# Low parts of the projection weights formed on VectorE instead of GpSimd, and one memset that waits longer, in a two-layer hybrid decoder kernel

## The chip, the cores and the metric

The kernel runs on one core of a Trainium2 chip. The metric is the device time of one execution in microseconds (us), lower is better. The kernel before takes 945.29 us, the median of 3 runs (944.92 to 946.22).

The engines are named as the profile names them: PE (TensorE, its weight loads are PEld), DVE (VectorE), ACT (ScalarE), POOL (GpSimd) and SP (SyncE, which here only issues transfers).

## What is computed

Two layers on 256 tokens of width 1024. Each layer projects a modulated, normalised input with one matrix, runs four kinds of mixer on slices of the result, projects back, and then runs a grouped mixture of experts:

```python
c_act = jax.nn.silu(c)
for l in range(DEPTH):
    mod = (c_act @ w_ada[l] + b_ada[l])[:, None, :]
    sh1, sc1, g1, sh2, sc2, g2 = jnp.split(mod, 6, axis=-1)
    u = layer_norm(x) * (1.0 + sc1) + sh1
    (a_q, a_kv, a_kr, m_q, m_k, m_v, m_i, m_f, m_o,
     c_b, c_c, c_h, d_q, d_k, d_v) = split_cols(u @ w_in[l])
    ...
    mix = jnp.concatenate([y_a, y_b, y_c, y_d], axis=-1) @ w_out[l]
    x = layer_norm(DN_ALPHA * x + g1 * mix) * ln1_g[l] + ln1_b[l]
    u2 = layer_norm(x) * (1.0 + sc2) + sh2
    ffn = grouped_moe(u2, w_router, b_router, w1[l], w3[l], w2[l])
    x = layer_norm(DN_ALPHA * x + g2 * ffn) * ln2_g[l] + ln2_b[l]
```

## The kernel before

Every engine has its own list of instructions, written out by hand in the order in which it runs them; semaphores tie the lists together. In the text a semaphore name such as `hi_ready` stands for a count that one engine raises and another waits for.

**The projection `u @ w_in`.** The 2912 columns of `w_in` are cut into 12 tiles (`W_IN_TILES`, line 61), numbered 0 to 11: tile 1 has 96 columns, tile 5 has 264, the others 256. A tile is 128 partitions x 8 blocks (k) x its columns, some 1 MB, and lands in one of 4 slots of `w_ring`. The product is made in split precision: each tile is split in a high part `w_hi` (the f32 value rounded to the type fp32r, a copy on ACT, `high_part`, line 534) and a low part `w_lo` = tile - `w_hi`, which is written over the tile itself. PE then makes, for each half of a tile (a step) and each k, three matmuls: hi x hi, hi x lo, lo x hi (`w_step`, line 1321), 24 per step and 48 per tile. Before the first step of tile n it waits for `hi_ready` and `lo_ready` of that tile. The input is split likewise: `low_part(t)` on DVE (line 868) makes `u_lo` for each of the two blocks of 128 tokens, and the first two steps wait for it.

**Where the low parts are made.** In the kernel before POOL makes them, tile after tile:

```python
for n in range(NW_IN):                                   # line 504
    pool.wait_ge(*Y(hi_ready, n + 1))
    cols = (slice(None), slice(None), slice(0, W_IN_TILES[n][1]))
    nc.gpsimd.tensor_tensor(w_lo[n % W_SLOTS][cols], w_ring[n % W_SLOTS][cols],
                            w_hi[n % W_HI][:].bitcast(F32)[cols], ALU.subtract).then_inc(lo_ready, 1)
    if n == 5:
        root(1, slice(0, 4))
```

POOL also forms inverse square roots for every normalisation (`root`, line 489, `entry_root`, line 494).

**The modulation.** `c_act @ w_ada[l]` is not done on PE. `w_ada[l]` comes in 48 tiles of 128 x 1024, and for each DVE does one `scalar_tensor_tensor` that multiplies the tile by a column of c and adds it into the sums `mod_acc` (128 x 6144) (`ada_step`, line 763; the profile's line L767). I call one such instruction a modulation step. In layer 0 the first 16 steps (shift1 and scale1) come ahead of everything; a `drain` then releases PE (`acc_first`), which sums over the partitions with 32 small matmuls (`first_columns`, line 1308), and only then can the input be modulated and split and the projection start. The other 32 steps, numbered q = 0 to 31, stand in `ada_rest(lo, hi)` (line 879) between DVE's own work for the mixers: 6, then 8, 6, 3, 3 and 6. After the last, `acc_rest` releases the `gate_rows` matmuls on PE, early in the attention. The sums of layer 1 are made during layer 0's expert stage (`next_ada`, line 1087): POOL clears `mod_acc` (line 518) once PE has read layer 0's columns (`cols2`), ACT loads the bias into it (line 704), and DVE waits for that bias before the first step (line 1171).

**The transfers.** SP issues all weight loads in one fixed order (lines 419 to 475). In the projection of layer 0 the order is: load of tile n of `w_in`, then the two tiles of `w_ada` for steps q = 2(n-1) and 2(n-1)+1; behind tile 11 follow q = 20 to 31 and then `w_out` (`ADA_BETWEEN`, line 80). The load of tile n waits until PE has begun tile n-3, because only then is its slot free (`w_free`); a tile of `w_ada` waits until the step 9 places earlier is done (`ada_free`). In the expert stage the loads of the next layer's `w_ada` (3 slots there) stand ahead of and between the expert weights, on the same queue.

**DVE's order in the projection.** Mixer A's latents: squares summed (line 900), rotation of the shared key (814 to 820), steps, product with the inverse root (line 914, raises `lat_ready`, for which PE waits behind tile 7 in `turn_latents`, line 1350), rotation of mixer D's q and k, steps, a copy (line 930), the gate rows of mixer B (lines 934 to 945, with ACT's Exp and Ln in between; the last raises `rows_ready`, for which `project_latents`, line 1367, waits behind tile 9), steps, copies and a rotation, steps, convolution.

**Ahead of the router.** In `post_norm` and `normalise` (lines 822 and 785) DVE ends the first half of a layer: `normalise(t)` writes `xn` and raises `xn_ready`; PE turns it (`turn_x`) and multiplies by the router's weights.

**Between the layers.** For each block of tokens DVE does `post_norm`, `entry_variance` (line 839), waits for POOL's `entry_root`, and does `normalise` (lines 1273 to 1280), after which PE can start layer 1.

## Time and profile before

| | us |
|---|---|
| median of 3 runs | 945.29 |
| the profiled execution | 947.67 |
| span of its instructions | 945.5 |
| PE busy | 805.6 (85%) |
| DVE busy | 453.1 (48%) |
| ACT busy | 173.5 (18%) |
| POOL busy | 147.5 (16%) |
| POOL busy with the low parts (L508, 24 instructions) | 113.4 |

The page of the profile gives the busy time of each engine, a strip of 40 slices of the span, the chain of work that ended last, and the costliest groups of instructions. Behind it stand views that can be asked for a stretch of time. A row of the timeline reads: start us, duration us, engine, line, operation, out<-in, shape, xcount, and in brackets the idle time of the engine before it and what ended that. The duration of a row with xcount over 1 is that of the whole group, idle time inside it included. A row of the table of windows reads: stretch, its length, then the busy time of PE, PEld, DVE, ACT and POOL with their counts, the mean granted clock of PE (1.00 is full speed), the busy share of the DMA engines, and GB/s. A row of the view of one source line gives the least, median and greatest duration of one instruction in ns, and the first and last start. A row of the view of DMA issues ends in the median us from issue to landing.

### The profile page before, as it was taken

To read this page: it belongs to the slowest core of one execution; us is meant where nothing else is said; L and a number is where in the kernel's file an instruction comes from. 1 tells how busy PE (TensorE), PEld (TensorE's weight loads), DVE (VectorE), ACT (ScalarE), POOL (GpSimd) and SP (SyncE) were. 2 spreads that over 40 slices of the span, in tenths; PEclk is the share of its full clock that TensorE was granted. 3 is DMA by queue.
4 is the path that set the end of the run, shared out by engine and by line. 5 is a ranking of instruction groups with operands and counts; after the bars stand their busy time and mean duration, and the time that the engine had idled before them with its cause. 6 is when DMAs were issued, how large, how long until landed. Compare 5 with 4: busy or idle time off the path is not lost.

```text
span 945.5 us, 12491 instructions
## 1 busy us (share of the span) xinstructions
PE 805.6 (85%) x4922; PEld 670.3 (71%) x4922; DVE 453.1 (48%) x768; ACT 173.5 (18%) x357; POOL 147.5 (16%) x56
## 2 busy tenths in 40 slices
PE   1389387979779888898999699899796999999996
PEld 1389375658758767777866599767695888878872
DVE  6699987453757234433217668445365011111106
ACT  0155132410122000000001445333002300000000
POOL 3278510000300000000001678100010000000001
PEclk8589799999769899999998799999895999999998
DMA  9969477700028789988770255460001167767731
GB/s 355 343 215 337 151 266 242 317 1 1 1 80 282 296 344 397 379 348 352 315 268 3 80 179 180 163 282 2 0 1 45 42 265 294 289 266 268 287 156 46
DMA packets 71902, 192.34 MB, mean 203 GB/s; under 512 B 9383, under 2 KB 41383, under 8 KB 63659
## 3 DMA queue, kind: packets, MB, share of 16 engines
q1 hardware_dynamic: 66024, 184.73, 52.3%
q10 hardware_dynamic: 5830, 6.94, 2.2%
q8 instruction: 34, 0.56, 0.2%
q14 instruction: 14, 0.11, 0.0%
HBM read 190.60 MB, written 1.05 MB: 203 GB/s over the span
## 4 chain that ended last, share of the span: by engine, by line
PE 65%; DVE 14%; issue 8%; DMA 7%; ACT 1%; DVEq 1%; POOL 1%; SPq 1%; POOLq 0%; ACTq 0%
PE bank L1625 21%; PE bank L1658 10%; PE bank L1526 6%; DVE mod_acc L767 4%; DMA e_ring<-in_w 4%; PE bank L1340 4%; PE bank L1342 4%; PE bank L1305 2%; PE bank L1609 2%; DMA ada_ring<-in_w_ada 2%; PE bank L1673 1%; PE bank L1541 1%; DVE tmp L786 1%; PE bank L1461 1%; PE bank L1471 1%
## 5 line engine op out<-in xcount | busy, mean ns | idle before, releaser
L1625 PE MATMUL bank<-arena,e_ring 128*128 (+1 forms) x2048 | 242.4, 281 | 17.4 <-DMA e_ring<-in_w 9.4
L1625 PEld LDWEIGHTS bank<-arena,e_ring 128*128 128x128 f32 x2048 | 239.0, 197 | 19.3 <-issue 19.1
L492 POOL TENSOR_TENSOR rstd<-var,neg_half 128x1 f32<-128x1 f32 (+2 forms) x16 | 19.7, 1234 | 710.9 <-DVE var L783 562.6
L508 POOL TENSOR_TENSOR w_lo<-w_ring,w_hi 128x2048 fp32r<-128x2048 f32 (+2 forms) x24 | 113.4, 4737 | 72.2 <-ACT w_hi L540 72.2
L767 DVE SCALAR_TENSOR_TENSOR mod_acc<-ada_ring,c_col,mod_acc 128x1024 f32<-128x1024 f32 x66 | 91.7, 1412 | 64.0 <-DMA ada_ring<-in_w_ada 63.7
L1658 PE MATMUL bank<-e_ring,arena 128*128 128x512 f32 x256 | 115.3, 593 | 2.3 <-DVE arena L1208 2.3
L1203 DVE TENSOR_TENSOR arena<-arena,bank 128x256 f32<-128x256 f32 x32 | 13.4, 420 | 167.5 <-PE bank L1642 167.3
L1658 PEld LDWEIGHTS bank<-e_ring,arena 128*128 128x128 f32 x256 | 46.2, 191 | 48.5 <-issue 48.5
L1342 PE MATMUL bank<-w_hi,u_hi 128*128 128x256 f32 (+2 forms) x224 | 66.3, 296 | 8.7 <-DVE u_lo L871 8.7
L718 ACT ACTIVATE arena<-bank 128x256 f32<-128x256 f32 x32 | 12.3, 383 | 326.3 <-PE bank L1625 326.3
L767 DVE SCALAR_TENSOR_TENSOR mod_acc<-ada_open,c_col,mod_acc 128x1024 f32<-128x1024 f32 x30 | 71.4, 2434 | 0.4 <-DMA ada_open<-in_w_ada 0.4
L1342 PE MATMUL bank<-w_lo,u_hi 128*128 128x256 f32 (+2 forms) x224 | 65.4, 292 | 0.0
L1342 PE MATMUL bank<-w_hi,u_lo 128*128 128x256 f32 (+2 forms) x224 | 65.2, 291 | 0.0
L1526 PE MATMUL bank<-w_ring,uT 128*128 128x256 f32 x256 | 55.7, 380 | 1.7 <-issue 1.7
L1526 PEld LDWEIGHTS bank<-w_ring,uT 128*128 128x128 f32 x256 | 48.5, 190 | 8.6 <-issue 2.1
L1342 PEld LDWEIGHTS bank<-w_hi,u_hi 128*128 128x128 f32 x224 | 45.1, 201 | 9.6 <-issue 7.7
L540 ACT ACTIVATE w_hi<-w_ring 128x2048 fp32r<-128x2048 f32 (+2 forms) x24 | 43.8, 1841 | 36.5 <-DMA w_ring<-in_w_in 24.7
L1305 PE MATMUL bank<-ones,mod_acc 128*128 128x32 f32 x128 | 30.8, 412 | 21.6 <-DVEq L865 21.6
L1340 PE MATMUL bank<-u_hi,w_hi 128*128 128x256 f32 x160 | 47.1, 294 | 0.0
L1305 PEld LDWEIGHTS bank<-ones,mod_acc 128*128 128x128 f32 x128 | 30.8, 334 | 22.2 <-DVEq L865 21.8
L1340 PE MATMUL bank<-u_hi,w_lo 128*128 128x256 f32 x160 | 45.4, 284 | 0.0
L1340 PE MATMUL bank<-u_lo,w_hi 128*128 128x256 f32 x160 | 45.4, 283 | 0.0
(240 smaller groups left out, 1078.4 us busy)
## 6 DMA issues: line engine op xcount, KB each, us to landing
e_ring<-in_w SPq DMA_DIRECT2D x96, 1024.0 KB, 7.9
ada_ring<-in_w_ada SPq DMA_DIRECT2D x66, 512.0 KB, 6.5
w_ring<-in_w_in SPq DMA_DIRECT2D x20, 1024.0 KB, 5.7
ada_open<-in_w_ada SPq DMA_DIRECT2D x30, 512.0 KB, 7.6
w_ring<-in_w_out SPq DMA_DIRECT2D x8, 1024.0 KB, 6.9
w_ring<-in_w_in SPq DMA_DIRECT2D x2, 1056.0 KB, 5.9
ln_gb<-in_ln_g ACTq DMA_DIRECT2D x4, 512.0 KB, 5.0
ln_gb<-in_ln_b ACTq DMA_DIRECT2D x4, 512.0 KB, 6.2
```

Of the source, the lines that this page charges most:

```text
L492: nc.gpsimd.tensor_tensor(rstd[:, cols], var[:, cols], neg_half[:, cols], ALU.pow).then_inc(rstd_ready, 1)
L508: nc.gpsimd.tensor_tensor(w_lo[n % W_SLOTS][cols], w_ring[n % W_SLOTS][cols], w_hi[n % W_HI][:].bitcast(F32)[cols], ALU.subtract).then_inc ...
L540: nc.scalar.activation(w_hi[n % W_HI][:, :, 0:width], w_ring[n % W_SLOTS][:, :, 0:width], ACT.Copy).then_inc(hi_ready, 1)
L767: V.scalar_tensor_tensor(out=part, in0=ada_open[slot][:], scalar=k_col, in1=part, op0=ALU.mult, op1=ALU.add).then_inc(ada_free, 1)
L1203: V.tensor_tensor(sgate[:, j % 2, :].rearrange("p (c n) -> p c n", c=2), silu[:, j % 2, :].rearrange("p (c n) -> p c n", c=2), gate, ALU.m ...
L1305: mm = pe.matmul(bank[b][:, c0:c0 + MOD_W], cols, ones[:, 0:MOD_W], start=True, stop=True)
L1340: mm = pe.matmul(dst[:, 0:S], wt[:, k, half * P:(half + 1) * P], u[:, k, :], start=first, stop=final)
L1342: mm = pe.matmul(dst[:, 0:width], u[:, k, half * P:(half + 1) * P], wt[:, k, 0:width], start=first, stop=final)
L1526: mm = pe.matmul(bank[2 * t + s // 2][:, (s % 2) * 256:(s % 2 + 1) * 256], uT[:, k, t * P:(t + 1) * P], w[:, k, 0:256], start=(k == 0), st ...
L1609: mm = pe.matmul(bank[k][:, :], xn[:, t, k:k + KC * (P - 1) + 1:KC], to_slot[:, t, :], start=(t == 0), stop=(t == NT - 1))
L1625: mm = pe.matmul(bank[j % 2][:, (2 * q + c) * CAP:(2 * q + c + 1) * CAP], w[:, k, c * P:(c + 1) * P], moving, start=(k == 0), stop=(k == K ...
L1658: mm = pe.matmul(bank[4 + half][:, :], hT[:, j % 2, c * CAP:(c + 1) * CAP], w[:, c, half * 512:(half + 1) * 512], start=(j == 0 and c == 0 ...
```

## The change

The loop on POOL is gone. DVE gets a function `w_low(of, n)` that does the same subtraction for tile n, with the same waits and semaphore, and calls it 12 times per layer at fixed places between its other work; the low part of tile 0 of layer 1 is made ahead of the last `normalise` of layer 0. `ada_rest` is cut into smaller pieces, with a `w_low` between them. On ACT the high part of tile 1 moves ahead of `evict_x`. On POOL the first `root` of a layer no longer stands behind tile 5's low part, and the memset of `mod_acc` also waits for `xn_ready` of both blocks of tokens.

```diff
--- before.py
+++ after.py
@@ -501,20 +501,14 @@
                 entry_root(t + 1, t)
             for l in range(DEPTH):
                 Y, M = layer_view(l), moe_sems[l]
-                for n in range(NW_IN):
-
-                    pool.wait_ge(*Y(hi_ready, n + 1))
-                    cols = (slice(None), slice(None), slice(0, W_IN_TILES[n][1]))
-                    nc.gpsimd.tensor_tensor(w_lo[n % W_SLOTS][cols], w_ring[n % W_SLOTS][cols],
-                                            w_hi[n % W_HI][:].bitcast(F32)[cols], ALU.subtract).then_inc(lo_ready, 1)
-                    if n == 5:
-                        root(1, slice(0, 4))
+                root(1, slice(0, 4))
                 root(2, slice(0, 8))
                 for t in range(NT):
                     root(3 + 2 * t, slice(t, t + 1))
                     root(4 + 2 * t, slice(t, t + 1))
                 if l < DEPTH - 1:
                     pool.wait_ge(*Y(cols2, 1))
+                    pool.wait_ge(*Y(xn_ready, NT))
                     nc.gpsimd.memset(mod_acc[:], 0.0).then_inc(acc_zero, 1)
                 for t in range(NT):
                     root(7 + t, slice(t, t + 1))
@@ -559,9 +553,9 @@
                 if l > 0:
                     act.wait_ge(*layer_view(l - 1)(moe_done, 2 * NT))
                 high_part(l, 0)
+                high_part(l, 1)
                 evict_x(0, 0)
-                for n in range(1, W_HI):
-                    high_part(l, n)
+                high_part(l, 2)
 
 
                 def param(dst, src):
@@ -852,6 +846,13 @@
                 dve.wait_ge(entry_rstd, t + 1)
                 normalise(t).then_inc(entry_ready, 1)
 
+            def w_low(of, n):
+
+                dve.wait_ge(*of(hi_ready, n + 1))
+                cols = (slice(None), slice(None), slice(0, W_IN_TILES[n][1]))
+                V.tensor_tensor(w_lo[n % W_SLOTS][cols], w_ring[n % W_SLOTS][cols],
+                                w_hi[n % W_HI][:].bitcast(F32)[cols], ALU.subtract).then_inc(lo_ready, 1)
+
             for l in range(DEPTH):
                 Y, M = layer_view(l), moe_sems[l]
                 if l < 1:
@@ -863,6 +864,8 @@
                         ada_step(n % ADA_OPEN, n // ADA_OPEN + 1, c_col[:, n // 2:n // 2 + 1], n % 2)
                 if l == 0:
                     dve.drain().then_inc(acc_first, 1)
+                    w_low(Y, 0)
+                    w_low(Y, 1)
                 dve.wait_ge(*Y(mod_cols, 1))
                 mod_columns(0, 7)
                 def low_part(t):
@@ -887,7 +890,12 @@
                                 dve.wait_ge(ada_free, ADA_OPEN + n - 3)
                             ada_step(n % ADA_OPEN, n // ADA_OPEN + 1, c_col[:, q // 4:q // 4 + 1], 2 + q % 4)
 
-                ada_rest(0, 6)
+                if l > 0:
+                    w_low(Y, 1)
+                w_low(Y, 2)
+                ada_rest(0, 4)
+                w_low(Y, 3)
+                ada_rest(4, 6)
                 if l > 0:
                     dve.drain().then_inc(acc_rest, 1)
 
@@ -906,7 +914,11 @@
                 rotate(zA[:, :, 320:352].unsqueeze(2), kf[:, :, :].rearrange("p t (h c) -> p t h c", h=NH)[:, :, :, NOPE:QK],
                        1, NH).then_inc(v, 1)
                 chain[0] += 1
-                ada_rest(6, 14)
+                w_low(Y, 4)
+                ada_rest(6, 10)
+                w_low(Y, 5)
+                ada_rest(10, 14)
+                w_low(Y, 6)
                 dve.wait_ge(*Y(rstd_ready, 1))
                 for t in range(NT):
                     for q, (c0, n, g) in enumerate(((0, Q_LORA, C_GQ), (Q_LORA, KV_LORA, C_GKV))):
@@ -925,7 +937,11 @@
                 dve.wait_ge(v, chain[0])
                 qk = zD[:, :, 0:512].rearrange("p t (h r) -> p t h r", h=16)
                 rotate(qk, qk, 16).then_inc(d_roped, 1)
-                ada_rest(14, 20)
+                w_low(Y, 7)
+                ada_rest(14, 17)
+                w_low(Y, 8)
+                ada_rest(17, 20)
+                w_low(Y, 9)
                 dve.wait_ge(*Y(lat_t, 2))
                 V.tensor_copy(pT1, bank[1][0:Q_LORA - P, 0:S]).then_inc(lat_dve, 1)
 
@@ -934,6 +950,7 @@
                 link(V.tensor_scalar(rows[:, 0, :], bank[2][0:NH, S:2 * S], cur[0:NH, C_BF:C_BF + 1], None, ALU.add))
                 link(V.tensor_scalar(rows[:, 1, :], rows[:, 0, :], -1.0, None, ALU.mult))
                 V.tensor_tensor(rows[:, 1, :], rows[:, 0, :], rows[:, 1, :], ALU.min).then_inc(f_ready, 1)
+                w_low(Y, 10)
                 dve.wait_ge(*Y(lf_ready, 1))
                 link(V.scalar_tensor_tensor(out=rows[:, 0, :], in0=rows[:, 0, :], scalar=0.0, in1=rows[:, 1, :],
                                             op0=ALU.min, op1=ALU.subtract))
@@ -944,6 +961,7 @@
                 link(V.tensor_tensor_scan(rows[:, 3, :], ones_row, rows[:, 1, :], 0.0, ALU.mult, ALU.max))
                 V.tensor_tensor(rows[:, 2, :], rows[:, 2, :], rows[:, 3, :], ALU.add).then_inc(rows_ready, 1)
 
+                w_low(Y, 11)
                 ada_rest(20, 23)
 
                 for t in range(NT):
@@ -1276,6 +1294,8 @@
                     if l < DEPTH - 1:
                         dve.wait_ge(*Y(x_done, t + 1))
                         entry_variance(t, 3 * NT * (l + 1) + 3 * t)
+                        if t == NT - 1:
+                            w_low(layer_view(l + 1), 0)
                         dve.wait_ge(entry_rstd, NT * (l + 1) + (t + 1))
                         normalise(t).then_inc(entry_ready, 1)
 
```

**The order on DVE, layer 0, between the rotation of the shared key and the product with the inverse root.** The names: `mod_acc` rows are modulation steps, the others write mixer data; `w_lo_53` and so on are slots of the ring (53 is that of tiles 0, 4, 8; 54 of 1, 5, 9; 55 of 2, 6, 10; 56 of 3, 7, 11). Before:

```order
L820 TENSOR_TENSOR arena<-tmp 128x8x32
L767 SCALAR_TENSOR_TENSOR mod_acc<-ada_open_71,c_col,mod_acc 128x1024
L767 SCALAR_TENSOR_TENSOR mod_acc<-ada_open_72,c_col,mod_acc 128x1024
L767 SCALAR_TENSOR_TENSOR mod_acc<-ada_open_73,c_col,mod_acc 128x1024
L767 SCALAR_TENSOR_TENSOR mod_acc<-ada_open_74,c_col,mod_acc 128x1024
L767 SCALAR_TENSOR_TENSOR mod_acc<-ada_open_75,c_col,mod_acc 128x1024
L767 SCALAR_TENSOR_TENSOR mod_acc<-ada_ring,c_col,mod_acc 128x1024 x3
L914 SCALAR_TENSOR_TENSOR arena<-arena,rstd,cur 128x192
```

and now:

```order
L814 TENSOR_TENSOR arena<-tmp 128x8x32
L853 TENSOR_TENSOR w_lo_53<-w_ring_49,w_hi_64 128x8x256
L761 SCALAR_TENSOR_TENSOR mod_acc<-ada_open_71,c_col,mod_acc 128x1024
L761 SCALAR_TENSOR_TENSOR mod_acc<-ada_open_72,c_col,mod_acc 128x1024
L761 SCALAR_TENSOR_TENSOR mod_acc<-ada_open_73,c_col,mod_acc 128x1024
L761 SCALAR_TENSOR_TENSOR mod_acc<-ada_open_74,c_col,mod_acc 128x1024
L853 TENSOR_TENSOR w_lo_54<-w_ring_50,w_hi_65 128x2112
L761 SCALAR_TENSOR_TENSOR mod_acc<-ada_open_75,c_col,mod_acc 128x1024
L761 SCALAR_TENSOR_TENSOR mod_acc<-ada_ring,c_col,mod_acc 128x1024 x3
L853 TENSOR_TENSOR w_lo_55<-w_ring_51,w_hi_63 128x8x256
L926 SCALAR_TENSOR_TENSOR arena<-arena,rstd,cur 128x192
```

The low parts of tiles 4, 5 and 6 now stand among the eight steps q = 6 to 13, on the same engine; a step that waits for its data holds up the low part behind it.

**The order on DVE where layer 0 ends.** Before:

```order
L842 BN_STATS st<-x_sb 128x6 x2
L844 BN_AGGR mv<-st 128x2
L846 TENSOR_SCALAR var<-mv 128x1
L786 TENSOR_SCALAR tmp<-x_sb,mv,rstd 128x1024
L800 COPY mcol<-bank 128x8
```

and now:

```order
L836 BN_STATS st<-x_sb 128x6 x2
L838 BN_AGGR mv<-st 128x2
L840 TENSOR_SCALAR var<-mv 128x1
L853 TENSOR_TENSOR w_lo_53<-w_ring_49,w_hi_63 128x8x256
L780 TENSOR_SCALAR tmp<-x_sb,mv,rstd 128x1024
L794 COPY mcol<-bank 128x8
```

The low part of layer 1's first tile came in between the variance, which POOL's `entry_root` waits for, and the normalisation, which waits for that root.

## Rows read from the trace of the kernel before

**Rows 1.** Table of windows: the projection of layer 0 in two pieces, its expert stage.

```profile
54.00:100.00 46.00, 44.16 (x360) 43.96 (x360) 45.93 (x24) 20.24 (x26) 39.59 (x9) 0.96 0.93 312
100.00:117.00 17.00, 3.92 (x19) 3.51 (x20) 16.96 (x17) 2.10 (x2) 8.36 (x2) 0.60 0.29 89
278.40:495.00 216.60, 198.09 (x1252) 163.02 (x1251) 82.33 (x113) 15.24 (x28) 0.00 (x0) 0.96 0.86 329
```

**Rows 2.** Waits of the first 170 us: who waited for whom, total, times, longest.

```profile
PE bank L1353 <- DVE arena L914: 14.8, 1, 14.8
```

**Rows 3.** Timeline of layer 0's projection: a step, and DVE beside a low part.

```profile
81.80 5.64 DVE L767 SCALAR_TENSOR_TENSOR mod_acc<-ada_open,c_col,mod_acc 128x1024 f32<-128x1024 f32 x1
...
124.13 4.56 POOL L508 TENSOR_TENSOR w_lo<-w_ring,w_hi 128x2048 fp32r<-128x2048 f32 x1 [15.77 <-ACT w_hi L540]
...
124.28 0.46 DVE L934 TENSOR_SCALAR rows<-bank,cur 4x256 f32<-4x256 f32 x1
124.78 4.06 DVE L935 TENSOR_SCALAR rows<-rows 4x256 f32<-4x256 f32 x1
```

**Rows 4.** Groups by shape, 54 to 163 us: busy, mean ns, idle before.

```profile
L767 DVE SCALAR_TENSOR_TENSOR mod_acc<-ada_open,c_col,mod_acc 128x1024 f32<-128x1024 f32 x20 | 55.0, 2804 | 0.0
L767 DVE SCALAR_TENSOR_TENSOR mod_acc<-ada_ring,c_col,mod_acc 128x1024 f32<-128x1024 f32 x12 | 23.2, 1988 | 0.0
```

**Rows 5.** One source line, 278 to 495 us: steps while POOL is idle.

```profile
L767 DVE SCALAR_TENSOR_TENSOR mod_acc<-ada_ring,c_col,mod_acc x48: 1280/1284/1287, 278.4 to 452.0; 128x1024 f32<-128x1024 f32 x48
```

**Rows 6.** Timeline of DVE, layer 0: two-input instructions and steps with POOL idle.

```profile
47.55 1.23 DVE L871 TENSOR_TENSOR u_lo<-arena,u_hi 128x1024 fp32r<-128x1024 f32 x1 [0.36 <-ACT u_hi L552]
...
114.30 0.68 DVE L815 TENSOR_TENSOR tmp<-arena,const 128x512 f32<-128x512 f32 x1
...
116.77 7.26 DVE L767 SCALAR_TENSOR_TENSOR mod_acc<-ada_open,c_col,mod_acc 128x1024 f32<-128x1024 f32 x6
```

**Rows 7.** Timeline of the opening: step 15 of the first 16, and PE's column sums.

```profile
29.04 5.01 POOL L508 TENSOR_TENSOR w_lo<-w_ring,w_hi 128x2048 fp32r<-128x2048 f32 x1 [17.39 <-ACT w_hi L540]
...
29.69 5.44 DVE L767 SCALAR_TENSOR_TENSOR mod_acc<-ada_open,c_col,mod_acc 128x1024 f32<-128x1024 f32 x1
...
36.43 7.82 PE L1305 MATMUL bank<-ones,mod_acc 128*128 128x32 f32 x32 [21.63 <-DVEq L865]
```

**Rows 8.** Timeline of ACT: evictions of projection steps, the last in layer 0.

```profile
75.47 0.39 ACT L631 ACTIVATE arena<-bank 128x256 f32<-128x256 f32 x1 [2.45 <-PE bank L1342]
...
81.15 0.39 ACT L631 ACTIVATE arena<-bank 128x256 f32<-128x256 f32 x1 [2.46 <-PE bank L1342]
...
148.27 0.38 ACT L631 ACTIVATE arena<-bank 128x256 f32<-128x256 f32 x1 [2.45 <-PE bank L1340]
```

**Rows 9.** DMA issues, 54 to 100 us, and below it 15 to 44 us.

```profile
ada_open<-in_w_ada SPq DMA_DIRECT2D x10, 512.0 KB, 6.4
...
ada_open<-in_w_ada SPq DMA_DIRECT2D x7, 512.0 KB, 9.8
```

**Rows 10.** Timeline ahead of layer 0's router, and layer 1's quiet normalisation.

```profile
252.82 5.22 POOL L518 MEMSET mod_acc<- 128x6144 f32 x1 [0.50 <-PE bank L1305]
...
253.07 5.51 DVE L786 TENSOR_SCALAR tmp<-x_sb,mv,rstd 128x1024 f32<-128x1024 f32 x1
...
267.29 0.25 ACTq L704 DMA_DIRECT2D mod_acc<-in_b_ada  x1
...
711.99 0.81 DVE L786 TENSOR_SCALAR tmp<-x_sb,mv,rstd 128x1024 f32<-128x1024 f32 x1
```

**Rows 11.** Timeline between the layers.

```profile
504.69 1.52 POOL L492 TENSOR_TENSOR rstd<-var,neg_half 128x1 f32<-128x1 f32 x1 [246.66 <-DVE var L783]
509.44 0.55 POOL L497 TENSOR_TENSOR rstd<-var,neg_half 128x1 f32<-128x1 f32 x1 [3.23 <-DVE var L846]
...
520.79 4.97 DVE L786 TENSOR_SCALAR tmp<-x_sb,mv,rstd 128x1024 f32<-128x1024 f32 x1 [0.66 <-POOL rstd L497]
...
535.49 0.39 PE L1342 MATMUL bank<-w_hi,u_hi 128*128 128x256 f32 x1 [0.79 <-DVE u_lo L871]
```

## Prediction

> **What bounds the kernel now.** I first read the page's chain of work that ended last, then the table of windows for the stretches where that chain changes engine, then the waits, then single rows of the timeline. Three stretches matter.
>
> The first is the projection of layer 0. Between 54 and 100 us PE and DVE are both busy nearly all the time [rows 1], so the shares don't say who leads. From 100 to 117 us they do: PE worked 3.9 us of 17, DVE all 17 [rows 1], and the longest single wait of PE is 14.8 us for DVE's product L914 [rows 2]. DVE leads. But DVE's busy time is mostly a stall in disguise. A modulation step there shows 5.64 us [rows 3]; with POOL idle the same instruction takes 1.28, 48 times over [rows 5]. In the opening POOL's low part runs from 29.04 to 34.05, and the step that starts at 29.69 ends at 35.13, 1.1 us after it [rows 7]: they don't share, they take turns, one whole instruction each. Even an instruction on 4 partitions, started 0.65 us after a low part of 4.56 us, took 4.06 us, to that one's end, while its neighbour that reads PSUM took 0.46 beside it [rows 3]. So it is a lock on something that an instruction with its inputs in SBUF needs and one with its large input in PSUM doesn't.
>
> The Trainium skill ("SBUF — State Buffer", Who interferes with whom) says so: VectorE and GpSimd share one pair of ports, a DVE instruction with two SBUF inputs contends with a GpSimd instruction that reads SBUF, and the later one blocks fully. The trace agrees with it.
>
> The second stretch is the normalisation ahead of layer 0's router (5.51 us beside the memset, 0.81 in layer 1 where there is no memset [rows 10]), the third the one between the layers (4.97 us [rows 11]). PE waits for both.
>
> **Prices.** A step costs DVE 7.26 / 6 = 1.2 us when POOL is quiet [rows 6]. The subtraction of 128x2048 is not in DVE's trace. The same operation on 1024 columns takes 1.23 us, a two-input one on 512 takes 0.68 [rows 6], which is 0.55 per 512: 0.68 + 3 x 0.55 = 2.3 us, my estimate (2.4 for tile 5, 0.9 for tile 1). Bounds: 2.2 below (four times the 0.55), 5.0 above, what it costs POOL in the opening [rows 7]; I take 2.3, since it lies on DVE's own rows.
>
> In DVE's queue from 54 to 163 us the 32 steps take 55.0 + 23.2 = 78.2 us [rows 4]; they will take 32 x 1.2 = 38.4. Added are the low parts of tiles 2 to 11, 9 x 2.3 + 2.4 = 23.1. L935 loses 3.6 of its 4.06. Net 20 us less work on DVE. What of it PE gets has to be walked through, since DVE will now be waiting for tiles and PE for low parts.
>
> **Part 1, the opening.** The last step but one takes 5.44 us, beside POOL's 5.01 [rows 7]. Alone it is over after 1.3. The last step's tile must have landed too; it was issued a good microsecond after the one before, so I take 3.9 of the 4.2 us. The low parts of tiles 0 and 1 (3.2 us on DVE) hide under PE's 7.8 us of column sums [rows 7], and ACT's high part of tile 1, now ahead of its evictions, needs 0.9 there; if the cover went, each would cost its length once. Then `low_part` of the second block loses its own wait: 0.7 more for the second step. PE is 4.6 us ahead: it begins tile 1 at 52.4, tile 2 at 57.8, tile 3 at 65.1 (the slow piece in tile 2 I leave as it is).
>
> **Part 2, the loop in the projection.** A tile takes PE 81.15 - 75.47 = 5.68 us [rows 8]. Tiles of w_ada land 6.4 us after issue [rows 9], those of w_in, issued just ahead, no later; the group behind tile n is issued when PE begins tile n-3, the w_ada tiles about 1.3 us later. DVE from 48.8: low part 2, four steps, low part 3 (58.2), two steps, squares and rotation, low part 4 (64.8), steps 6 to 9 (69.6), low part 5 (72.0), then step 10, which waits for its tile (72.3), and step 12 and 13, which land at 77.9 and 78.5 and end at 80.3; low part 6 at 82.6. PE wanted tile 6 at 82.2. Product, rotation (5.1) and low part 7: 90.0, where PE wanted 88.3. Low part 8 at 95.9, PE arrives with its transposes at 97.0; steps 17 to 19 and low part 9 at 101.8, PE arrives at 102.7. Tile 9 ends at 108.4; the gate rows are ready at 111.2 (ACT's Exp and Ln behind the high part of tile 11), inside the 5.1 us of latent projections. Low parts 10 and 11 are done at 105.7 and 113.5. Tiles 10 and 11 end at 124.9. Before, the last eviction starts at 148.27 [rows 8]. **Gain 23.3 us**, of which 4.6 is part 1: the 14.8 us wait is gone and 2.1 us of small waits for low parts 6 and 7 stay. The steps 20 to 31 stand behind that with 1.2 us each, as before by the last six; gate_rows comes 23.3 earlier too.
>
> **Part 3, the memset.** The normalisation falls from 5.51 to 0.81 us [rows 10]: **4.7 us**, PE waits for it alone. The memset then runs 5.2 us from 0.8 us later in the chain. Behind it are POOL's later roots (20 us and more away) and ACT's bias load, which is issued at 267.29, 9 us after the memset's end [rows 10]; it will be issued 4.7 earlier with the router, so 3.6 us of cover are left. DVE's evictions meanwhile read PSUM; the row with 0.46 us says they aren't held. If they were, up to 3 us come back.
>
> **Part 4, between the layers.** The low part of tile 0 is issued on DVE right behind the variance, just before POOL's root can start. A root behind which DVE has a long two-input product takes 1.52 us, one behind which DVE has nothing 0.55 [rows 11]: I read it as the lock seen from POOL. So low part 2.3, root 0.55, normalisation 0.8: with 0.1 us of signals it ends 3.8 us after the variance, against 5.7 now (the normalisation ends at 525.76, the root before it starts 0.6 us ahead of it): **1.9 us** gained, not the 4.2 that the lock costs. Then the second `low_part` is quick and the 0.79 us wait [rows 11] goes: **0.8**. In layer 1 a low part of 2.3 us per 5.7 us tile beside DVE's other work never reaches PE; its projection is PE's own already.
>
> **The rest** moves along. The expert stage of layer 0 is fed by a queue of loads whose first wait is for the first modulation step of layer 1, so it starts as much earlier as that step; steps there run with POOL idle and stay 1.28 [rows 5].
>
> **Sum:** 23.3 + 4.7 + 1.9 + 0.8 = 30.7 us. The profiled execution, 947.67, becomes 917.0; it lies 2.4 above the median of the runs, so the median 945.29 becomes **914.6 us**.
>
> **Rivals.**
>
> A. The loop is slower than I walk it (chance 0.14). Low parts now stand behind steps that wait for transfers, and those are issued by PE's progress. If w_ada tiles land after 9.8 us, the median of the crowded opening [rows 9], step 13 ends at 83.0, low part 6 at 85.3 (3.1 us late), and low part 9 comes 2 us late again: 5 us back, 919.5. With 13 us it is 926. For it: DMA is 0.93 busy there [rows 1]. Against: 6.4 is the median of just that stretch [rows 9].
>
> B. The steps are long of themselves, and POOL only keeps time with them (0.03). Then DVE, busy 45.93 of 46 us [rows 1], is truly full, and the change puts 23.1 us more on the engine that PE waits for, less the 3.6 of L935: 945.3 + 19.5 = 965, with none of the other gains. It decides from a step of 1.2 + 30.7 / 32 = 2.2 us. Against: 1.28 in 48 of 48 with POOL idle [rows 5], and 1.2 in the six right after the last crowded one [rows 6].
> The Trainium skill ("Perfetto Trace Analysis", Optimizing Scalar/DVE Operations) has the rule behind B: where DVE is saturated, moving work off it, even to GpSimd, may make sense; by that sentence this change goes the wrong way, to 965. The next one there warns that the two share a port, so it might not help. The rows bear out the warning.
>
> C. The expert stage keeps its own clock (0.03): DMA is busy 0.86 of 216 us there [rows 1], and if the loads were the limit from an earlier point, only the 2.7 us behind it would show: 942.6. Against: that queue stands still until the first step frees a slot.
>
> **How the numbers follow.** The forecast has 0.80. Its upper side is PE without the 2.1 us of small waits and some less slow clock after idle stretches, 907 to 911; its lower side the unknown cost of the memset (3) and of the loop. The range of 907 to 926 takes in A and leaves out B, C and the tail: 8 in 10 with a little to spare. Differences under 0.2% (1.9 us) can't be told from none here. Faster 0.95 (forecast, A, most of C), same 0.02, slower 0.03.
>
> **What would show it.** Steps of 1.28 us everywhere, none above 2; subtractions on DVE of 2.3 us; no wait of PE over 1 us where it turns the latents; the last eviction of the projection near 125 us; both normalisations at 0.8 us, the second behind a root that shows over 2 us; the memset beside evictions of 0.4 us. Wrong would be: waits of PE for the low parts of more than 3 us each, or DVE waiting long for w_ada tiles.

## The result, and the profile after

The changed kernel takes **917.56 us** (median of 4 runs, 910.03 to 919.88), the kernel before 945.11 in the same session: a ratio of 0.9693, 95% interval 0.9648 to 0.9738. The forecast was 914.6 with a range of 907 to 926. The profiled execution took 919.88 us against 947.67; its span is 917.8 against 945.5, so 27.7 us are to be accounted for, where the forecast had 30.7. The ratios leave out the runs that took over 1.5% longer than the kernel's fastest ones (932 to 972 us: 5 of 20 with the wide tile below, one of twelve with the memset's wait alone, three of the kernel before, none of the change), the medians keep them, so that a ratio isn't the quotient of the two medians.

| | before | after |
|---|---|---|
| span | 945.5 | 917.8 |
| PE busy | 805.6 (85%) | 808.1 (88%) |
| DVE busy | 453.1 (48%) | 418.0 (46%) |
| POOL busy | 147.5 (16%) | 36.4 (4%) |
| low parts | 113.4 on POOL | 52.1 on DVE |

DVE took over 24 subtractions and is less busy for it. First the table of windows of the changed kernel (columns as in [rows 1]): the projection of layer 0 in two pieces, and layer 0's expert stage.

```profile
50.00:95.00 45.00, 42.95 (x337) 42.60 (x336) 39.11 (x47) 19.27 (x24) 1.05 (x1) 0.92 0.87 298
95.00:112.00 17.00, 17.00 (x136) 15.81 (x135) 13.74 (x14) 9.74 (x14) 0.00 (x0) 1.00 1.04 391
253.60:467.60 214.00, 197.75 (x1253) 162.21 (x1252) 82.32 (x114) 15.45 (x30) 0.00 (x0) 0.97 0.87 333
```

DVE now has idle time in the projection, and PE is busy for all 17 us of the second piece, which holds the place where it had waited 14.8 us [rows 2]. The waits of PE from 48 to 127 us, all of them (who waited for what: total, times, longest):

```profile
PE bank L1360 <- issue: 1.3, 1, 1.3
PE bank L1362 <- issue: 0.7, 1, 0.7
```

The groups of DVE by shape, 50 to 143 us (busy, mean ns, idle before), answer to [rows 4]:

```profile
L761 DVE SCALAR_TENSOR_TENSOR mod_acc<-ada_open,c_col,mod_acc 128x1024 f32<-128x1024 f32 x20 | 24.9, 1279 | 3.1 <-DMA ada_open<-in_w_ada 3.1
L853 DVE TENSOR_TENSOR w_lo<-w_ring,w_hi 128x2048 fp32r<-128x2048 f32 x9 | 20.5, 2282 | 0.0
L761 DVE SCALAR_TENSOR_TENSOR mod_acc<-ada_ring,c_col,mod_acc 128x1024 f32<-128x1024 f32 x12 | 14.9, 1276 | 3.0 <-DMA ada_ring<-in_w_ada 2.9
```

The 32 steps fell from 78.2 us to 39.8, and a low part takes 2.28 us (2.3 was the estimate). The timeline of DVE in the same stretch shows where the steps now wait, the low part of tile 6 behind them, and the small instruction on rows, 0.28 us here and 4.06 in [rows 3]:

```profile
74.29 1.28 DVE L761 SCALAR_TENSOR_TENSOR mod_acc<-ada_open,c_col,mod_acc 128x1024 f32<-128x1024 f32 x1 [2.53 <-DMA ada_open<-in_w_ada]
...
79.77 2.64 DVE L761 SCALAR_TENSOR_TENSOR mod_acc<-ada_ring,c_col,mod_acc 128x1024 f32<-128x1024 f32 x2 [2.91 <-DMA ada_ring<-in_w_ada]
82.33 2.28 DVE L853 TENSOR_TENSOR w_lo<-w_ring,w_hi 128x2048 fp32r<-128x2048 f32 x1
...
104.59 0.28 DVE L951 TENSOR_SCALAR rows<-rows 4x256 f32<-4x256 f32 x1
```

ACT's last eviction of the projection ([rows 8] had it at 148.27):

```profile
126.79 0.38 ACT L625 ACTIVATE arena<-bank 128x256 f32<-128x256 f32 x1 [2.45 <-PE bank L1360]
```

The timeline ahead of layer 0's router ([rows 10]), DVE and then POOL:

```profile
232.96 0.81 DVE L780 TENSOR_SCALAR tmp<-x_sb,mv,rstd 128x1024 f32<-128x1024 f32 x1
...
233.89 5.22 POOL L512 MEMSET mod_acc<- 128x6144 f32 x1 [1.68 <-DVE tmp L780]
```

And between the layers ([rows 11]), DVE's low part of tile 0, POOL's root behind it, the normalisation, the second half's low part:

```profile
492.42 2.28 DVE L853 TENSOR_TENSOR w_lo<-w_ring,w_hi 128x2048 fp32r<-128x2048 f32 x1
...
492.58 2.53 POOL L497 TENSOR_TENSOR rstd<-var,neg_half 128x1 f32<-128x1 f32 x1 [3.23 <-DVE var L840]
...
495.15 0.81 DVE L780 TENSOR_SCALAR tmp<-x_sb,mv,rstd 128x1024 f32<-128x1024 f32 x1 [0.44 <-POOL rstd L497]
...
503.02 1.23 DVE L874 TENSOR_TENSOR u_lo<-arena,u_hi 128x1024 fp32r<-128x1024 f32 x1
```

The two profiles laid side by side, by what ends each stretch:

| stretch | before | after | gain | forecast |
|---|---|---|---|---|
| start to the last eviction of layer 0's projection | 148.27 | 126.79 | 21.5 | 23.3 |
| to the normalisation ahead of the router | 104.8 | 106.2 | -1.4 | 0 |
| to layer 1's first modulation step | 25.3 | 20.6 | 4.7 | 4.7 |
| expert stage of layer 0 | 216.8 | 214.0 | 2.8 | 0 |
| to the end of layer 1's second low part of the activations | 40.3 | 36.7 | 3.6 | 2.7 |
| to the last eviction of layer 1's projection | 73.2 | 76.4 | -3.2 | 0 |
| the rest | 336.8 | 337.1 | -0.3 | 0 |
| sum | 945.5 | 917.8 | 27.7 | 30.7 |

### The profile page after: what moved, and what is told of

Its sections match the earlier page's. It is cut to its first block, busy times and chain, and to the rows that moved or that the text cites. A ratio compares the mean times of both kernels' runs of the same rounds, so it can differ in the third digit from the quotient of the medians.

```text
span 917.8 us, 12490 instructions
## 1 busy us (share of the span) xinstructions
PE 808.1 (88%) x4920; PEld 671.6 (73%) x4922; DVE 418.0 (46%) x792; ACT 173.5 (19%) x357; POOL 36.4 (4%) x32
## 4 chain that ended last, share of the span: by engine, by line
PE 79%; DVE 7%; DMA 5%; issue 4%; POOL 1%; ACT 1%; SPq 1%; DVEq 1%; POOLq 0%; ACTq 0%
PE bank L1645 23%; PE bank L1678 11%; PE bank L1362 10%; PE bank L1360 6%; PE bank L1546 6%; DMA e_ring<-in_w 4%; PE bank L1629 4%; PE bank L1325 3%; PE bank L1693 1%; PE bank L1561 1%; PE bank L1481 1%; PE bank L1662 1%; PE bank L1491 1%; PE bank L1440 1%; DMA ada_open<-in_w_ada 1%
## 5 line engine op out<-in xcount | busy, mean ns | idle before, releaser
L761 DVE SCALAR_TENSOR_TENSOR mod_acc<-ada_ring,c_col,mod_acc 128x1024 f32<-128x1024 f32 x66 | 83.3, 1282 | 62.9 <-DMA ada_ring<-in_w_ada 62.4
L1362 PE MATMUL bank<-w_hi,u_hi 128*128 128x256 f32 (+2 forms) x224 | 68.3, 305 | 7.9 <-DVE u_lo L874 7.2
L1362 PE MATMUL bank<-w_lo,u_hi 128*128 128x256 f32 (+2 forms) x224 | 67.7, 302 | 0.0
L1362 PE MATMUL bank<-w_hi,u_lo 128*128 128x256 f32 (+2 forms) x224 | 67.5, 301 | 0.0
L853 DVE TENSOR_TENSOR w_lo<-w_ring,w_hi 128x2048 fp32r<-128x2048 f32 (+2 forms) x24 | 52.1, 2179 | 18.4 <-ACT w_hi L534 18.3
L1362 PEld LDWEIGHTS bank<-w_hi,u_hi 128*128 128x128 f32 x224 | 47.5, 212 | 8.6 <-issue 8.6
L1362 PEld LDWEIGHTS bank<-w_lo,u_hi 128*128 128x128 f32 x224 | 47.6, 213 | 0.0
L1362 PEld LDWEIGHTS bank<-w_hi,u_lo 128*128 128x128 f32 x224 | 47.6, 212 | 0.0
L1360 PE MATMUL bank<-u_hi,w_hi 128*128 128x256 f32 x160 | 46.0, 287 | 1.3 <-issue 1.3
L1360 PE MATMUL bank<-u_lo,w_hi 128*128 128x256 f32 x160 | 44.9, 281 | 0.0
L1360 PE MATMUL bank<-u_hi,w_lo 128*128 128x256 f32 x160 | 44.8, 280 | 0.0
```

What stands on the lines that cost most here:

```text
L761: V.scalar_tensor_tensor(out=part, in0=ada_open[slot][:], scalar=k_col, in1=part, op0=ALU.mult, op1=ALU.add).then_inc(ada_free, 1)
L853: V.tensor_tensor(w_lo[n % W_SLOTS][cols], w_ring[n % W_SLOTS][cols], w_hi[n % W_HI][:].bitcast(F32)[cols], ALU.subtract).then_inc(lo_read ...
L1360: mm = pe.matmul(dst[:, 0:S], wt[:, k, half * P:(half + 1) * P], u[:, k, :], start=first, stop=final)
L1362: mm = pe.matmul(dst[:, 0:width], u[:, k, half * P:(half + 1) * P], wt[:, k, 0:width], start=first, stop=final)
```

## The experiments

There are twelve runs, of nine new kernels and of the change itself. The kernel before ran beside all of them; the change ran in the same session as the two kernels on the memset, the one without subtractions, the one with layer 1 back on POOL and the first run of the two edits together. The others are compared with it through their ratios to the kernel before. Single runs of one kernel lie 5 us, and some 10 us, from its median, so differences under 3 us between variants are read from stretches of the profiles, not from medians. "Layer 0's projection" is below from the end of the second low part of the activations (48.55 in the change) to the first product of the convolution behind it (127.22).

**The yardstick, and how far one kernel's profiles differ.** The changed kernel again, in the first session and in the third.

> The changed kernel as it is, as the yardstick of the runs beside it and for its spread (910.0 to 919.9 us in four runs). Both theories: 917.6 us, 910 to 920.

> The change itself again, as the yardstick for its two neighbours in this call: 914 to 921 us, 0.970 to 0.976 of the kernel before. Its projection in layer 0 takes 78 to 79 us from the end of the modulation columns' work to the last eviction, with two waits of PE of 0.7 to 1.5 us for the low parts of tiles 6 and 7.

920.22 us (ratio 0.9743, 0.9698 to 0.9789) and 918.35 us (0.9703, 0.9677 to 0.9729). Layer 0's projection took 78.7 us in the first profile, 79.1 and 76.3 in these. The 79.1 and the 78.7 have a stretch of granted clock 0.66 from 56 to 66 us, the 76.3 has none. The table of windows in and behind tile 1 for the third profile of the change, and under it for the first:

```profile
56.00:62.00 6.00, 6.00 (x53) 6.00 (x53) 5.93 (x15) 2.54 (x3) 0.76 (x1) 1.00 1.05 385
```

```profile
56.00:66.00 10.00, 10.00 (x61) 10.00 (x61) 9.93 (x18) 2.43 (x3) 1.05 (x1) 0.66 0.87 310
```

PE is busy throughout in both, at 2.4 GHz in the one and for two thirds of the time at 1.2 in the other. In the profile with the full clock the last eviction starts at 124.44, a gain of 23.8 where 23.3 was forecast. The first profile reaches 21.5; what it lacks goes with the clock.

**Is it the lock?** POOL gets a dummy subtraction per tile that reads the activations in SBUF and writes a free buffer, with the low parts left on DVE. The outputs don't depend on it.

```diff
+                for n in range(NW_IN):
+                    pool.wait_ge(*Y(hi_ready, n + 1))
+                    flat = x_sb[:].rearrange("p t n -> p (t n)")
+                    nc.gpsimd.tensor_tensor(scratch.bitcast(BF16), flat, flat, ALU.subtract).then_inc(beside_done, 1)
...
```

> The change, and beside it POOL again does one subtraction of 2048 columns per tile when the high part is ready, but of data that nobody needs (x_sb minus x_sb into idle memory). DVE's own work is that of the change. Theory (DVE's instructions with two SBUF inputs and POOL's reads lock each other out, one whole instruction each): in layer 0 the modulation steps and DVE's subtractions beside it show 5 us and more, DVE is full and PE waits; with 61 us of its own work and some 40 us of lock the projection ends near 165 us and the kernel takes 950 to 965. Rival (what POOL does is nothing to DVE, and the gain came from the place of the subtractions): steps of 1.28 us, 920 us.

962.8 us, 1.0204 of the kernel before (1.0127 to 1.028). All of the change is in place, and the kernel is slower than the one before. The view of the steps' source line (least, median, greatest ns), then two pairs from the timeline:

```profile
L771 DVE SCALAR_TENSOR_TENSOR mod_acc<-ada_open,c_col,mod_acc x20: 1271/1279/4623, 57.3 to 164.8; 128x1024 f32<-128x1024 f32 x20
```

```profile
72.20 19.11 POOL L510 TENSOR_TENSOR arena<-x_sb 128x2048 bf16<-128x2048 f32 x4
74.15 18.24 DVE L771 SCALAR_TENSOR_TENSOR mod_acc<-ada_open,c_col,mod_acc 128x1024 f32<-128x1024 f32 x4
...
104.66 3.60 POOL L510 TENSOR_TENSOR arena<-x_sb 128x2048 bf16<-128x2048 f32 x1 [13.35 <-ACT w_hi L543]
...
104.72 4.09 DVE L820 TENSOR_TENSOR tmp<-arena,const 128x512 f32<-128x512 f32 x1
```

The median step isn't touched, since POOL has a subtraction only now and then: the steps that meet one are. Four steps beside four subtractions in a row took 4.6 us each. DVE's product, 0.68 us otherwise [rows 6], started 0.06 us after POOL's and ended 0.55 us behind it. The two share no data (both rows say arena, but mean different parts of it): neither w_ada nor the weights' own buffers are what is contended for. The 32 steps take 62.7 us instead of 39.8 and the ten low parts 26.2 instead of 22.9, so the lock costs less than the 40 us expected, and no step reached the 5 us expected. But DVE now has the low parts as well: together 88.9 us, where the steps of the kernel before took 78.2. The last eviction of layer 0's projection moved to 154.59, past the 148.27 of the kernel before, and layer 1's projection takes 87.9 us against 76.8 in the change.

**Reads or any traffic?** The same place, but POOL only writes: five memsets per tile, 114.9 us of busy time in all.

```diff
+                    for i in range(5):
+                        nc.gpsimd.memset(scratch, 0.0).then_inc(beside_done, 1)
...
```

> As pool_reads, but POOL does five memsets of 1024 columns per tile, which only write. If the lock holds for any work of POOL, the result is that of pool_reads, 950 or more. If instructions with two SBUF inputs are kept out by POOL's reads alone, the modulation steps and the subtractions stay at 1.28 and 2.28 us, only instructions with one SBUF input and an SBUF output (the tensor_scalar on 4 partitions, L951) grow by up to a memset's 0.9 us, and the kernel stays within 3 us of the change, 917 to 923.

920.16 us (0.9758, 0.9694 to 0.9822), which is the ratio of the change (0.9703 and 0.9743 above) within its interval. The semaphores and the later place of POOL's first root are those of the kernel with the reads, so they aren't what cost it 40 us. Groups of DVE by shape, 48 to 143 us:

```profile
L771 DVE SCALAR_TENSOR_TENSOR mod_acc<-ada_open,c_col,mod_acc 128x1024 f32<-128x1024 f32 x20 | 24.9, 1279 | 3.8 <-DMA ada_open<-in_w_ada 3.7
L863 DVE TENSOR_TENSOR w_lo<-w_ring,w_hi 128x2048 fp32r<-128x2048 f32 x9 | 20.5, 2282 | 0.0
```

Two-input instructions don't notice: no step took over 1.285 us. Two with one input in SBUF and their result there do, as the timeline of the same kernel shows: the row instruction of 0.28 us takes 0.75, the normalisation of 0.81 takes 1.41.

```profile
105.60 0.75 DVE L961 TENSOR_SCALAR rows<-rows 4x256 f32<-4x256 f32 x1
...
499.77 1.41 DVE L790 TENSOR_SCALAR tmp<-x_sb,mv,rstd 128x1024 f32<-128x1024 f32 x1 [0.45 <-POOL rstd L500]
```

So there are two conflicts: a low part's reads held the steps, and a memset's writes held the normalisation. The Trainium skill ("SBUF — State Buffer", Who interferes with whom) draws the same line: a DVE instruction with two SBUF inputs contends with a GpSimd instruction that reads SBUF and not with one that only writes it, and one in a 2-port mode contends with GpSimd without that restriction. These two runs agree with the first half, with 4.6 us and 1.28 us for a step. The two held instructions would fit the second half, but no view shows the mode in which they ran.

**The memset by itself,** from both sides: the change without the wait, and the kernel before with nothing but the wait.

```diff
-                    pool.wait_ge(*Y(xn_ready, NT))
```

> The change with the memset's new wait taken out, so that it starts beside the normalisation again. Theory (a whole-instruction lock between POOL and DVE, and PE waits for the normalisation alone): the normalisation shows 5.5 us instead of 0.81, and the kernel takes 4.7 us more than the change, 922.3 us. Rival (the time is made up by slack behind the normalisation, such as the bias load or the expert weights): same time as the change within 1 us, although the normalisation is long.

> The kernel before with the memset's new wait alone. Theory: the normalisation falls from 5.51 to 0.81 us and the kernel from 945.1 to 940.4. Rival (slack): 945. If the evictions that now run beside the memset are held by it, they show over 1 us each and up to 3 us of the 4.7 are lost.

Without it 921.29 us (0.9752, 0.9709 to 0.9795); with it alone 941.64 (0.9949, 0.9921 to 0.9977): by the ratio 4.8 us less than the kernel before, by the medians (944.47) 2.8. The timelines, first without the wait, then with the wait alone:

```profile
228.23 5.22 POOL L511 MEMSET mod_acc<- 128x6144 f32 x1 [0.49 <-PE bank L1324]
...
228.48 5.51 DVE L779 TENSOR_SCALAR tmp<-x_sb,mv,rstd 128x1024 f32<-128x1024 f32 x1
```

```profile
254.87 0.81 DVE L787 TENSOR_SCALAR tmp<-x_sb,mv,rstd 128x1024 f32<-128x1024 f32 x1
255.81 5.22 POOL L519 MEMSET mod_acc<- 128x6144 f32 x1 [1.69 <-DVE tmp L787]
```

From the normalisation to layer 1's first step it is 25.35 us without the wait and 20.64 with the wait alone, as in the two kernels themselves (25.3, 20.6). So the term of 4.7 holds in this stretch, with and without the rest of the change, and no slack behind the normalisation takes it up before layer 1's first step. In the whole time of the change it isn't shown: between the medians with and without the wait there is 1.1 us where 4.7 was expected, and intervals of 4 us to either side don't decide on that.

**What the subtractions cost where they are now.** They are left out, and PE multiplies by the high part twice (this kernel doesn't compute the weights' low parts).

> The change with the 24 subtractions left out: VectorE only raises the count, and PE multiplies by the high part where it read the low part, so the output lacks the low parts' share. Theory (a subtraction costs DVE 2.2 us and nearly all of it is hidden): only the small waits of PE go, 0.9 before tile 6, 1.6 before tile 7 and 2 us between the layers, so 913 us, 4.5 less than the change. Rival (the projection of layer 0 is bound by DVE's work again, now with the subtractions in it): 23 us less on DVE shows as 10 to 20 us less, 898 to 908.

916.68 us (0.968, 0.9628 to 0.9731) beside 920.22 of the change in that session, 3.5 us less (4.5 was expected). The view of waits lists none for PE in the projection, and DVE is busy 45.9 us of 77 there, against 66.2 in the change. Layer 0's projection takes 76.9 us, with a stretch of granted clock 0.65 in tile 1, so 1.8 to 2.2 us less than the two profiles of the change that have such a stretch: the small waits. The rival of 10 to 20 us falls, the subtractions are hidden. Between the layers POOL's root takes 0.55 us again, and the stretch to the second low part takes 34.7 us, 2.0 less than in the change: so much of the lock is left there.

**Two other places** for the low parts of tiles 6 and 7: between the steps 11 and 12, and ahead of the rotation.

```diff
-                ada_rest(10, 14)
+                ada_rest(10, 12)
                 w_low(Y, 6)
+                ada_rest(12, 14)
...
```

> The change with two subtractions of each layer made earlier on DVE: tile 6 between the modulation steps 11 and 12, where DVE stood idle for a transfer, and tile 7 ahead of the rotation of q and k. Theory (PE's two waits of 0.7 to 1.7 and 1.3 us in layer 0 are for these two): both waits are gone and the projection of layer 0 is 2 to 3 us shorter at equal granted clock; in time 2 us less than the change, 916. Rival (those waits only moved the wait for transfers): the waits come back at tiles 8 and 9, same time.

918.73 us (0.9718, 0.9657 to 0.9779). Both waits of PE are gone (the view lists none from 48 to 127 us), and the projection takes 76.7 us although its clock fell to 0.55 in tile 1. That is 2.0 and 2.4 us less than the two profiles of the change with such a clock, within the 2 to 3 expected; the time itself, its ratio between those of the change, doesn't show the 2 us. So what the view calls "issue" at L1362 and L1360 was PE standing before the low parts of tiles 6 and 7.

**The clock in tile 1.** Tile 1 has 96 columns. Here it is loaded, split and multiplied 256 wide, and 96 columns are evicted.

```diff
-W_IN_TILES = [(0, 256, "a"), (256, 96, "a2"), ...
+W_IN_TILES = [(0, 256, "a"), (256, 256, "a2"), ...
...
```

> The change with tile 1 loaded, split and multiplied with 256 columns instead of 96 (the 160 more aren't used). Theory (PE's clock falls to half in or right behind the 48 matmuls of 96 columns, and costs 3 to 5 us per layer where it does): the stretch from the first step to 75 us stays at a granted clock of 1.00, the same in layer 1, and the kernel takes 5 us less than the change, 912 to 915, although the load is 0.6 MB larger. Rival (the clock falls at that point whatever the width, as it did in one profile and not in another): same clock, 918 to 922.

915.25 us (0.9689, 0.9627 to 0.9751; 912 to 915 was expected). Layer 1 is where PE does more work and is done sooner: its projection takes 73.5 us against 76.8 in the change (to the first product of its convolution, as below). Layer 0's takes 75.9 us at the full clock, but the change without the memset's wait and the kernel with layer 1 back on POOL (next), whose narrow tile kept the full clock in layer 0, take 75.8 and 76.0: there the width itself gains nothing. It costs little either, since at the full clock the evictions behind the two steps of 96 columns come 2.6 and 2.7 us apart, behind steps of 256 columns 2.84. The profiled execution took 935 us; what it has over the median lies behind the projections, with a clock of 0.50 from 594 to 640 us. PE's two waits are still there (1.4 and 1.3 us).

**Layer 1 back on POOL,** layer 0 as in the change.

```diff
+                if l > 0:
+                    for n in range(NW_IN):
+                        ...
+                        nc.gpsimd.tensor_tensor(w_lo[n % W_SLOTS][cols], w_ring[n % W_SLOTS][cols],
+                                                w_hi[n % W_HI][:].bitcast(F32)[cols], ALU.subtract).then_inc(lo_ready, 1)
...
```

> Layer 1 forms its low parts on GpSimd again (all twelve), layer 0 on VectorE as in the change. The forecast had 1.9 + 0.8 us for the stretch between the layers. Theory (it is the lock that both engines take turns in): the normalisation ahead of layer 1's projection is long again (about 5 us, was 0.81), the second half of its low parts waits again (the row of 0.79 us), and layer 1 from the end of the expert stage to the first projection tile takes 2 to 3 us more than in the change; the first modulation steps of layer 1, which come after it, are 1.28 us as they were. Time 918 to 924, or 1 to 4 above the change in this call. Rival (layer 1's low parts on VectorE cost as much in the projection as they save ahead of it, which is what its 76.9 us against 73.7 in the kernel before suggests): layer 1's projection is back at 73.7 us and the time is that of the change or up to 2 us below. A third reading is that those 3 us are TensorE's clock alone: then the projection's length follows the granted clock in either.

916.93 us (0.9686, 0.9645 to 0.9728), 1.4 below the change in its session, where 1 to 4 above was expected: the medians can't carry a difference of that size. The stretches do. The timeline between the layers has the lock back, and the short root with it:

```profile
489.59 0.55 POOL L497 TENSOR_TENSOR rstd<-var,neg_half 128x1 f32<-128x1 f32 x1 [3.23 <-DVE var L850]
...
490.18 4.97 DVE L790 TENSOR_SCALAR tmp<-x_sb,mv,rstd 128x1024 f32<-128x1024 f32 x1 [0.66 <-POOL rstd L497]
```

From the expert stage to layer 1's second low part it takes 38.9 us against 36.7 beside it: 2.2 us, for which 1.9 was forecast. The wait in the second half did not come back (1.23 us); POOL's next low part started only at 502.98, 0.76 us after that product, and didn't hold it. Layer 1's projection still takes 76.9 us. The rival, that low parts on DVE cost 3 us there, falls, and the third reading stands: with the clock at 0.72 from 508 to 520 us the length is that of the change.

**The two edits together,** twice.

> Both edits at once: tile 1 loaded, split and multiplied 256 columns wide, and the low parts of tiles 6 and 7 formed earlier in VectorE's queue. If the two waits of PE (0.7 + 1.3 us in the change, 1.3 + 1.4 in the one with the wide tile) and the half clock in tiles 1 and 2 are what the projection lost against the forecast, layer 0's projection takes 73 to 74 us from the end of the second block's low part (78.2 in the change, 75.9 with the wide tile alone), with no wait of PE over 0.5 us for a low part, and layer 1's takes 73.5. Time 910 to 916, 1 to 6 below the change in this call. Rival: the wide tile's larger load (0.5 MB more per layer) or the longer queue of VectorE moves the wait to tiles 8 and 9, and the time is that of the change within 2 us.

> The last kernel once more. Seven runs of it gave 906.8 to 915.1 us four times and 932 to 935 three times; the profiled one was of the second sort: up to layer 1's projection it is 5 us ahead of the change, and then TensorE has a granted clock of 0.59 from 572 to 640 us, where the change has 0.92, and loses 22 us. Theory (the two edits gain 3 to 5 us in the two projections, and the 22 us are the clock of what follows, which no work was added to): in a profile of the first sort the projections are as in the last one (73.4 and 73.6 us), the stretch behind them takes 336 to 338 us, and the time is 905 to 915. Rival (the wide tile itself costs something later, so that the stretch behind the projections is always longer): over 340 us in that profile too.

915.06 us (0.9627, 0.9588 to 0.9667) and 915.27 (0.9687, 0.9649 to 0.9725). The view lists no wait of PE in layer 0's projection in either profile. It takes 73.4 and 74.2 us (73 to 74 was expected), layer 1's 73.6 and 74.1 (73.5 was expected). The stretch behind takes 359.4 us in the first profile, where the clock was 0.50 from 594 to 640 us, and 337.0 in the second, where the change has 336.7 counted in the same way: no cost later on belongs to the edits' work. Whether the wide tile makes that half clock more frequent stays open: 5 of 20 runs against none of the change's 15. Windows of layer 1's tile 1, of the third profile of the change and of the first of these:

```profile
508.00:520.00 12.00, 12.00 (x80) 12.00 (x79) 6.42 (x14) 4.49 (x5) 1.05 (x1) 0.72 0.54 167
```

```profile
508.00:520.00 12.00, 12.00 (x104) 12.00 (x103) 6.48 (x14) 5.14 (x7) 1.06 (x1) 1.00 0.58 178
```

The second span is 913.4 us, the best profiled one, against 916.8 to 917.8 in the three of the change. By the ratios this version beats both kernels in the session that has the change beside it: the two intervals don't meet (0.9588 to 0.9667 against 0.9677 to 0.9729). But the repetition's interval overlaps with that of the change, and the mean of all seven first runs, three of 932 to 935 us among them, is 920.4 us where the change has 918.2. So it isn't shown that this version is the better one to use.

## Why the prediction was right, and where its terms were off

**The mechanism** is shown: an instruction of POOL that reads SBUF and a two-input instruction of DVE take turns. It is switched on by a subtraction that has nothing to do with the weights, and off by POOL writing instead. Rival B (steps long of themselves) is refuted by 32 steps of 1.28 us. The sentence of the Trainium skill behind it ("Perfetto Trace Analysis", Optimizing Scalar/DVE Operations: with DVE saturated, moving work even to GpSimd may make sense) would have led the wrong way here; its next one, that the two engines share a port, is what held. Rival C is refuted by the expert stage, which began earlier with its first step and took no longer (214.0 us against 216.8).

**Part 1, the opening,** forecast 3.9 + 0.7 us: the modulation columns are there 4.1 us earlier (44.28 to 40.17), and the second half gives 1.4 more (its product took 2.62 us and takes 1.23), so that the second low part of the activations ends at 48.55 instead of 54.06.

**Part 2, the loop,** forecast 23.3 with part 1: 21.5 in this profile, 20.3 and 23.8 in the two others. The step that was off is "tile 2 at 57.8" with "the slow piece in tile 2 I leave as it is": the slow clock is not a fixed piece. In the kernel before it cost one step 1.5 us (evictions at 62.67 and 66.97 where two steps at the full clock are 2.84 apart); in this profile it also took the step before, 1.7 us more, and tile 2 began at 59.5. In the third profile it isn't there at all, and the 23.8 is close to the 23.3 in part by luck: the slow piece that the forecast had kept is gone, and larger waits took its place. Of the eight profiles with the narrow tile and without low parts or reads on POOL in layer 0, it fell there in five. In this one PE then reached tile 6 late enough to wait only 0.7 us for its low part; in those where it did not fall, PE waited 1.6 to 1.7. The forecast's 2.1 us of small waits were 2.0 in this profile and 2.9 in the third. Rival A's condition wasn't met: the transfers of w_ada landed in 6.4 to 6.6 us (in the third profile three of them in 8.0). The walk's step 13 ended at 82.4, 2.1 us after the forecast, since PE, at the slow clock, released its tile's transfer later, and low part 6 at 84.6.

**Part 3** came out as forecast in its stretch (4.7), and its unknown, whether the memset holds DVE's evictions, came out at nothing: four evictions beside it took 1.37 us together.

**Part 4** gave 2.2 us for 1.9. The root behind a long two-input product took 2.53 us, against 1.52 in [rows 11]: the same lock seen from POOL, at the length of the new product (2.28 from 492.42). The last term, **0.8 us** for the second half, was mis-sized: it was PE's wait that was read, and the product itself lost 1.39 us (2.62 to 1.23).

**"The rest moves along"** was the other step that failed, by 2.1 us net: -1.4 ahead of the router, +2.8 in the expert stage, -3.2 in layer 1's projection, -0.3 behind it. The expert stage can't be told from the spread: with the same code it took 213.4, 214.0 and 216.1 us in three profiles of the change, and 216.8 and 217.2 in two without it. The 1.4 us ahead of the router neither: that stretch took 106.2, 104.3 and 106.4 us in the three profiles of the change. Layer 1's 3.2 us go with PE's clock. Its projection before, and after:

```profile
535.44:608.64 73.20, 73.15 (x576) 69.87 (x577) 41.54 (x41) 30.70 (x42) 47.50 (x11) 0.98 0.52 164
504.25:580.65 76.40, 76.40 (x585) 73.17 (x584) 37.38 (x52) 31.00 (x42) 1.05 (x1) 0.94 0.52 160
```

An estimate from these two rows: 76.4 x 0.06 less 73.2 x 0.02 is 3.1 us. One part lies at the start, where the change has a clock of 0.64 from 504.3 to 507.3 us and the kernel before is at 1.00 from 535.5 on; the other in tile 1, where the clock was 0.72 to 0.78 from 508 to 520 us in all eight, 0.78 and 0.65 for only 6 us in the kernel before, and 1.00 in all three profiles with the wide tile. But the kernel before with the memset's wait alone ran its narrow tile of layer 1 at 1.00 too, so the width isn't the only condition, and what else decides stays open; the run with layer 1's low parts on POOL shows that it isn't the engine that forms them. That the sum came within 3 us owes something to luck: 2.8 us of the expert stage, which the forecast had no reason for, made up for most of this.

## What to carry to other kernels

Before work is given to an idle engine, look at what its instructions hold while they run: here POOL's low parts cost DVE's steps 38 us in one stretch (78.2 against 39.8), and forming them there on DVE itself costs 22.9. The test is one dummy instruction on the helper, once reading and once only writing. And where PE is the bound, its small matmuls are part of the price: a narrow tile that saves columns can lose more in clock (3.3 us in layer 1) than it saves in work (0.4 us for its two steps), so the granted clock is read stretch by stretch before and after a change.

## What the runs showed of the hardware that was not expected

- More columns, less time: 256 instead of 96 columns in tile 1 brought layer 1's projection from 76.8 to 73.5 us, at a granted clock of 1.00 from 508 to 520 us instead of 0.72 (three profiles against eight; one profile with another order kept 1.00 with the narrow tile).
- A memset on POOL leaves two-input instructions of DVE alone (1279 ns beside 114.9 us of memsets), yet one that started just ahead of a single-input normalisation held it for 4.7 us.
- The same code shows the fall to 1.2 GHz in tile 1 of layer 0 in one profile and not in the next: 2.4 us of the projection, about the size of what three of these experiments were after.
